# Gate and up projections as Strassen's seven half-size products, in two passes with partial results in DRAM

## What is computed

```python
x = x + (mix @ w_out[l]).astype(x.dtype)
x = x + swiglu(rmsnorm(x, norm2_w[l]), w_gate_up[l], w_down[l]).astype(x.dtype)
...
def swiglu(h, w_gate_up, w_down):
    gu = h @ w_gate_up
    gate, up = jnp.split(gu, 2, axis=-1)
    return (jax.nn.silu(gate) * up) @ w_down
```

## Time and profile before

| | us |
|---|---|
| median of 3 runs | 2583.36 (2579.16 to 2587.95) |
| the profiled execution | 2588.09 |
| its span, first to last instruction | 2586.3 |

### The profile page before, as it was taken

How to read it: one execution, slowest core, us unless ns; L and a number is a source line. 1 busy time by engine, 2 the same in 40 slices (tenths; PEclk the granted TensorE clock), 3 DMA queues, 4 the chain that set the end, 5 groups by cost and what they waited for, 6 DMA issues and landing times.

```text
span 2586.3 us, 36373 instructions
## 1 busy us (share of the span) xinstructions
PE 2475.5 (96%) x15138; PEld 2063.7 (80%) x15138; DVE 1193.8 (46%) x2105; ACT 558.7 (22%) x905; POOL 477.6 (18%) x162
## 2 busy tenths in 40 slices
PE   6899999998999999999999999989999999999998
PEld 6778888887788788888787877777778888888887
DVE  6884138873698523141622733663522222222224
ACT  4211111214321102141323434430210000000002
POOL 2100232230000132202210100000333333333330
PEclk8989999999999999999999999999999999999999
DMA  8544534236466833421333431123111111111101
GB/s 268 151 154 153 175 109 136 82 114 204 135 208 208 252 118 130 140 100 62 122 109 117 144 116 71 69 70 124 49 49 49 49 49 49 49 45 45 44 20 65
DMA packets 226899, 284.69 MB, mean 110 GB/s; under 512 B 31857, under 2 KB 144466, under 8 KB 226770
## 3 DMA queue, kind: packets, MB, share of 16 engines
q1 hardware_dynamic: 194370, 234.44, 28.2%
q10 hardware_dynamic: 32400, 48.38, 5.1%
HBM read 200.89 MB, written 81.89 MB: 109 GB/s over the span
## 4 chain that ended last, share of the span: by engine, by line
PE 82%; DVE 9%; DMA 3%; issue 3%; ACT 3%; SPq 1%; POOL 0%; ACTq 0%; DVEq 0%; POOLq 0%
PE PS L500 26%; PE PS L3127 19%; PE PS L503 16%; PE PS L3144 9%; DVE W_LO L409 1%; PE PS L1854 1%; PE PS L1834 1%; DMA LAR<-ret_d 1%; PE PS L682 1%; PE PS L2421 1%; PE PS L2416 1%; PE PS L1174 1%; DMA CB<-pch_d 1%; DVE XN L643 1%; PE PS L1295 1%
## 5 line engine op out<-in xcount | busy, mean ns | idle before, releaser
L442 POOL TENSOR_SCALAR W_HI<-RAW 128x2048 fp32r<-128x2048 f32 (+1 forms) x66 | 132.1, 2011 | 1507.7 <-PE PS L500 671.8
L500 PE MATMUL PS<-W_HI,OP_HI 128*128 128x512 f32 (+1 forms) x1184 | 310.2, 406 | 5.3 <-DVE XI L1458 2.9
L500 PE MATMUL PS<-W_LO,OP_HI 128*128 128x512 f32 (+1 forms) x1184 | 292.1, 389 | 0.0
L500 PE MATMUL PS<-W_HI,OP_LO 128*128 128x512 f32 (+1 forms) x1184 | 289.1, 387 | 0.0
L500 PEld LDWEIGHTS PS<-W_HI,OP_HI 128*128 128x128 f32 x1184 | 222.1, 196 | 53.7 <-issue 4.7
L500 PEld LDWEIGHTS PS<-W_LO,OP_HI 128*128 128x128 f32 x1184 | 223.2, 192 | 46.8 <-issue 0.5
L500 PEld LDWEIGHTS PS<-W_HI,OP_LO 128*128 128x128 f32 x1184 | 220.4, 189 | 44.6 <-issue 0.3
L3200 DVE TENSOR_TENSOR AB<-PS,GSB 128x512 f32<-128x512 f32 x44 | 30.4, 691 | 391.0 <-ACT GSB L3183 391.0
L529 ACT ACTIVATE OST<-PS 128x512 f32<-128x512 f32 (+2 forms) x164 | 91.2, 556 | 503.6 <-PE PS L503 269.1
L503 PE MATMUL PS<-OP_HI,W_HI 128*128 128x512 f32 (+1 forms) x768 | 190.8, 391 | 3.8 <-POOL W_HI L442 3.8
L503 PE MATMUL PS<-OP_HI,W_LO 128*128 128x512 f32 (+1 forms) x768 | 184.1, 382 | 0.3 <-DVE W_LO L409 0.3
(11 more groups left out here) (449 smaller groups left out, 3425.3 us busy)
## 6 DMA issues: line engine op xcount, KB each, us to landing
RAW<-in_w_in SPq DMA_DIRECT2D x28, 1024.0 KB, 5.9
RAW<-in_w_gate_up SPq DMA_DIRECT2D x44, 512.0 KB, 4.7
RAW<-in_w_out SPq DMA_DIRECT2D x12, 1024.0 KB, 8.9
RAWD<-in_w_down SPq DMA_DIRECT2D x11, 1024.0 KB, 4.9
X<-x_d SPq DMA_DIRECT2D x4, 2048.0 KB, 9.1
x_d<-X SPq DMA_DIRECT2D x2, 4096.0 KB, 16.5
ptok_d<-OST ACTq DMA_DIRECT2D x24, 256.0 KB, 2.0
pch_d<-OST ACTq DMA_DIRECT2D x24, 256.0 KB, 2.1
```

Of the source, the lines that this page charges most:

```text
L442: nc.gpsimd.tensor_scalar(hi, raw, 1.0, 1.0, ALU.mult, ALU.mult).then_inc(*w_hi.by(1))
L500: ins = nc.tensor.matmul(PS[:, bank, 0:width], act_part[:, k, (g.tile0 + a) * P:(g.tile0 + a + 1) * P], w_part[:, slot, k, 0:width], start ...
```

## The change

Gate and up are no longer computed as two products of full size. Of a block's weights, the gate and up columns (256 each) and the two halves of the contraction make a 2x2 matrix of blocks (`A11`, `A21` in rows 0 to 511, `A12`, `A22` in rows 512 to 1023), the activations another one (the two halves of the contraction, `K1` and `K2`, by the two halves of the tokens, `T1` and `T2`). Strassen's scheme in Winograd's form gets the four result blocks from seven products of half size. Each is 12 matmuls for each of the two column tiles `f`.

- First pass, over all 11 blocks: four products (regions 0 to 3 of `WRH`, `WRL`), 8 x 12 = 96 matmuls a block. Two of the weight operands are sums of blocks. The partial results, four kinds for each block, go to `spill_d` in DRAM, eight DMAs of 256 KB a block.
- Second pass, over all 11 blocks again, with the weights loaded again: three products, 6 x 12 = 72 matmuls a block, then the down product of 96 as before. All three weight operands are sums or differences of blocks, and the activations are three precomputed sums (`C1`, `C6`, `C7`, made in steps 1, 3, 5 and 7 of the first pass). The partial results are fetched back, four DMAs of 512 KB a block.
- DVE makes the sums of weight blocks in place in `RAW` (two or three of 128x1024), POOL rounds them to `WRH` (one of 128x1024 for each region), and DVE makes `WRL`, which POOL did before (`lo`). POOL also rounds `w_down`; DVE subtracts.
- A product's PSUM bank is copied by ACT, and a second product is then accumulated onto the same bank.
- The fifth normalization gets times of its own (`NORM5`). It subtracts one half of the features from the other, and six of its tiles are now transposed ahead of the first product of the layer, which is woven together with `out2`.

The diff, cut to what is spoken of:

```diff
+    NF = 2 * FFB
+    spill_d = scratch("spill_d", (4 * NF * P, HALF))
+    WRH, WRL = at("WRH", "whi", 16384, [P, 4, 4, 2 * P], F32R), at("WRL", "wlo", 16384, [P, 4, 4, 2 * P], F32R)
...
+    RAWD = at("RAWD", "ophi", 16384, [P, 2, D])
...
+    E_UP, E_GATE, UP1, GATE2 = range(4)
+    STEPS = 2 * FFB
+    SUM_TIMES = (1, 3, 5, 7)
...
     def sp_ffn(sp):
...
+        sp.wait_ge(*ff_lo(3))
+        load_half(1, 1)
+        for i in range(FFB):
+            sp.wait_ge(*ff_lo(region_no(i, 3)))
+            load_half(i + 1, 0)
+            for f in range(2):
+                sp.wait_ge(*ff_cp(8 * i + 3 + f))
+                store(UP1, i, f, UPC)
+            for f in range(2):
+                sp.wait_ge(*ff_q(4 * i + 1 + f))
+                store(E_UP, i, f, PRE)
+            sp.wait_ge(*ff_lo(region_no(i + 1, 2)))
+            load_half(i + 2, 1)
+            for f in range(2):
+                sp.wait_ge(*ff_cp(8 * i + 7 + f))
+                store(GATE2, i, f, GSI)
+                sp.wait_ge(*ff_q(4 * i + 3 + f))
+                store(E_GATE, i, f, POST)
+        sp.wait_ge(*products_done(FFB - 1, 6))
+        load_down(0)
+        for kind, tile in ((E_UP, LE1), (UP1, LUP), (GATE2, LGS), (E_GATE, LE2)):
+            sp.wait_ge(*ff_st[kind](16 * NF))
+            fetch(kind, 0, tile)
+        sp.wait_ge(*ff_lo(region_no(FFB, 2)))
+        load_half(FFB + 1, 0)
+        for i in range(FFB):
+            j = FFB + i
+            if i + 1 < FFB:
+                sp.wait_ge(*ff_wlo(i + 1))
+                load_down(i + 1)
+            if j + 2 < STEPS:
+                sp.wait_ge(*ff_lo(region_no(j + 1, 2)))
+                load_half(j + 2, 0)
+                load_half(j + 2, 1)
...
     def pool_ffn(pool):
+        def hi(j, r):
+            pool.wait_ge(*sums_done(j))
+            if j:
+                pool.wait_ge(*products_done(j - 1, 2 * r + 2))
+            else:
+                pool.wait_ge(*mm_done(gemms["out2"].first + 13))
+            G.tensor_scalar(WRH[:, r], region_source(j, r), 1.0, 1.0, ALU.mult, ALU.mult).then_inc(*ff_hi.by(1))
...
     def pe_ffn(pe):
+        def product(r, f, bank, hi, lo, ks, ts, clear):
+            for n, (w, x) in enumerate(((WRH, hi), (WRL, hi), (WRH, lo))):
+                for k in range(4):
+                    ins = nc.tensor.matmul(PS[:, bank, :], w[:, r, k, f * P:(f + 1) * P], x[:, ks + k, ts],
+                                           start=clear and n == 0 and k == 0, stop=n == 2 and k == 3, skip_group_check=not clear)
+            ins.then_inc(*ff_p.by(1))
...
     def dve_ffn(dve, chain):
...
+        def sums(j):
+            dve.wait_ge(*ff_raw[0](32 * (j + 1)))
+            dve.wait_ge(*ff_raw[1](32 * (j + 1)))
...
+        def lo(j, r):
+            dve.wait_ge(*ff_hi(region_no(j, r)))
+            V.tensor_tensor(WRL[:, r], region_source(j, r), WRH[:, r].bitcast(F32), SUB).then_inc(*ff_lo.by(1))
...
+        for j in range(FFB):
+            T = ff_time(j)
+            if j:
+                yield T + 0.3
+                lo(j, 3)
...
+            yield T + 1.7
+            sums(j + 1)
+            yield T + 2.3
+            lo(j + 1, 0)
+            yield T + 2.45
+            lo(j + 1, 1)
+            for f in range(2):
+                yield T + 2.7 + 0.5 * f
+                dve.wait_ge(*ff_cp(8 * j + 5 + f))
+                chain(V.tensor_tensor(POST[:, f, :], PRE[:, f, :], POST[:, f, :], ADD))
+                V.tensor_tensor(PRE[:, f, :], PS[:, f, :], POST[:, f, :], SUB).then_inc(*ff_q.by(1))
+            yield T + 3.35
+            lo(j + 1, 2)
...
+        for i in range(FFB):
+            j = FFB + i
+            T = ff_time(j)
...
+            V.tensor_tensor(WD_LO[:, :, :], RAWD[:, :, :], WD_HI[:, :, :].bitcast(F32), SUB).then_inc(*ff_wlo.by(1))
+            if i == 0:
+                yield T + 0.95
+                sums(j + 1)
...
+            for f in range(2):
+                yield T + 1.5 + 0.5 * f
...
+                dve.wait_ge(*products_done(j, 3 + f))
+                V.tensor_tensor(LE1[:, f, :], PS[:, f, :], LE1[:, f, :], ADD).then_inc(*ff_c11.by(1))
...
+                V.tensor_tensor(LE1[:, f, :], LE1[:, f, :], LUP[:, f, :], ALU.mult).then_inc(*ff_ab.by(1))
+                if f == 0 and j + 1 < STEPS:
+                    yield T + 2.25
+                    lo(j + 1, 1)
+                yield T + 2.15 + 0.4 * f
+                dve.wait_ge(*ff_ahi(4 * i + 1 + f))
+                V.tensor_tensor(A_LO[:, f, T1], LE1[:, f, :], A_HI[:, f, T1].bitcast(F32), SUB).then_inc(*ff_alo.by(1))
+            for f in range(2):
...
+                chain(V.tensor_tensor(LE2[:, f, :], PS[:, 2 + f, :], LE2[:, f, :], ADD))
+                V.tensor_tensor(LE2[:, f, :], LE2[:, f, :], LGS[:, f, :], ALU.mult).then_inc(*ff_ab.by(1))
...
+                V.tensor_tensor(A_LO[:, f, T2], LE2[:, f, :], A_HI[:, f, T2].bitcast(F32), SUB).then_inc(*ff_alo.by(1))
+                if f == 0 and j + 1 < STEPS:
+                    yield T + 3.3
+                    lo(j + 1, 2)
+            if i + 1 < FFB:
+                for v in range(15):
+                    yield T + 3.3 + 0.25 * v
+                    add(i, v)
+                    if v == 9 and j + 2 < STEPS:
+                        yield T + 5.6
+                        sums(j + 2)
...
+    NORM5 = (10.2, 11.2, 12.2, 13.2, 14.2, 15.2, 15.7, 16.7)
```

More of the change, by code:

```diff
@@ new lines, in region_source, with spill, load_half, load_down @@
+    def region_source(j, r):
+        return ((A21, A22, A12, A11) if first_part_of(j) else (A11, A12, A21))[r]
+    def spill(kind, f, n):
+        row = (kind * NF + f) * P
+        return spill_d[row:row + n * P, :]
+    def sp_ffn(sp):
+        def load_half(j, half):
+            i = j % FFB
+            for m in range(2):
+                src = wgu[half * HALF:(half + 1) * HALF, i * 256 + m * FF:i * 256 + m * FF + 256]
+                sp.dma_start(RAW[:, half, :, m * 256:(m + 1) * 256], src.rearrange("(k p) n -> p k n", p=P))\
+                  .then_inc(*ff_raw[half].by(16))
+        def load_down(i):
+            sp.dma_start(RAWD[:, :, :], wdn[i * 256:(i + 1) * 256, :].rearrange("(k p) n -> p k n", p=P))\
+              .then_inc(*ff_raw[2].by(16))
+        def store(kind, i, f, tile):
+            sp.dma_start(spill(kind, 2 * i + f, 1), tile[:, f, :]).then_inc(*ff_st[kind].by(16))
+        def fetch(kind, i, tile):
+            sp.dma_start(tile[:, :, :], spill(kind, 2 * i, 2).rearrange("(f p) n -> p f n", p=P))\
+              .then_inc(*ff_ld[kind].by(16))
+        sp.wait_ge(*w_split(len(halves)))
+        load_half(0, 0)
+        load_half(0, 1)
+        sp.wait_ge(*ff_lo(3))
[33 more added lines that the diff above has]
+            if i + 1 < FFB:
+                sp.wait_ge(*ff_alo(4 * i + 2))
+                fetch(E_UP, i + 1, LE1)
+                fetch(UP1, i + 1, LUP)
+                sp.wait_ge(*ff_alo(4 * i + 4))
+                fetch(GATE2, i + 1, LGS)
+                fetch(E_GATE, i + 1, LE2)
@@ L3115, in pool_ffn @@
+        for r in range(3):
+            hi(0, r)
+        for j in range(FFB):
+            hi(j, 3)
+            for r in range(3):
+                hi(j + 1, r)
+        for i in range(FFB):
+            j = FFB + i
+            pool.wait_ge(*ff_raw[2](16 * i + 16))
             if i:
@@ L3166, in pe_ffn @@
[L3166 to L3191 removed]
+                pool.wait_ge(*products_done(FFB, 0))
@@ L3209, in add @@
             V.tensor_tensor(X[:, t, c * HALF:(c + 1) * HALF], X[:, t, c * HALF:(c + 1) * HALF],
-                            PS[:, 4 + v % 4, :], ALU.add).then_inc(*ff_x.by(1))
-        dve.wait_ge(*xn_turned(turned_base(5) + TT))
-        with dve.Fori(0, FFB - 1) as i:
-            gate(i)
-            for v in range(16):
-                add(i, v)
-        gate(FFB - 1)
+                            PS[:, 4 + v % 4, :], ADD).then_inc(*ff_x.by(1))
+        yield 10.3
+        sums(0)
+        for r, time in enumerate((13.35, 13.75, 14.75, 15.65)):
+            yield time
+            lo(0, r)
```

402 lines of the change are left out of this document (282 added, 120 removed), and 2 rows, old and new, of the table SHARED.

## The result

The changed kernel takes 2602.06 us (median of 5 runs, 2595.43 to 2603.66) against 2583.36 before; the ratio is 1.0062, 95% interval 1.0047 to 1.0077. It is slower by 0.6%, where I had forecast 2576 us, faster by 0.3%. The time lies 1 us above my range of 2550 to 2601.

The account below looks back on a forecast made before the run. PE, busy 96% of the span, was taken as the bound. Terms -59.8 - 8 + 4 + 21 + 35 = -7.8 us took the profiled 2586.3 to 2578.5; allowing for the 2583.36 median, the forecast was 2576 us, range 2550 to 2601.

Parts of the forecast that it names:

- Beginning, -8: Start of the layer: POOL no longer subtracts there, so `XN` is not held up; 8 us saved, 2 of 10.0 kept.
- Arithmetic, -59.8: Eleven blocks: 264 matmuls fewer at 0.2267 us each save 59.8 us, if PE still never waits.
- First pass, +4 (0 to 15): First pass: the load loop of 22.1 us against 21.76 makes each step wait 0.4 us, 4 us over 11.
- The loop 13.9 + 3p: First pass, from step start until `ff_q` lets the next step start: 13.9 us + 3p, p the us for 1 MB.
- one of the rivals (0.13, 2598 us): First pass bound by its load loop: at p = 3.3 a step waits 2.1 us, 23 in all; chance 0.13.
- 1.8 + 3p = 10.0 us: Loop's middle: two 1 MB loads and 1 MB of spills, 3p = 8.2 us, then 1.8 us until landed.
- 8.4: Loop's last part: sums, two roundings, two `lo`, additions and hand-overs until `ff_q`, 8.4 us.
- 3.7: Loop's first part: from step start through partial results, rounding and `lo` to SP's issue of loads, 3.7 us.
- Port in the first pass: First-pass loop: two POOL roundings, 2.10 us, hold the port that DVE operations with two SBUF inputs need.
- Turn, +21 (14 to 26): First step of second pass: waits of 19.6 us before the first down product and 1.9 before down tile 4.
- Later steps, +35: Nine later second-pass steps: waits before down tiles 0 and 4, 3.9 us each step, 35 us (26 to 39).
- Clock: Rival: PE's clock falls after the wait for tile 4, 1.8 us for nine steps, +16, 2592 us; chance 0.13.

Follow-up runs that it names:

- e10: Changed kernel with only orders changed, on SP and VectorE, in first pass, turn and second pass; 2517.88 us, ratio 0.9747 to the kernel before.
- e8: Changed kernel with the four stores of the second half of a first-pass step issued by ScalarE into its own queue; 2581.92 us.
- e1: Changed kernel with the four GATE2 and E_GATE stores of a first-pass step queued on SP behind the next load of half 0; 2572.07 us.
- e2: Changed kernel with ScalarE, not GpSimd, rounding the WRH regions of steps 1 to 10 in the first pass; 2587.73 us.

## Why the prediction was wrong

- *Beginning, -8:* -11, of which 10 are the two waits and what follows them. Right in sign and near in size by luck, since the mechanism was wrong: not `XN`.
- *Arithmetic, -59.8:* as said; e10 shows it whole.
- *First pass, +4 (0 to 15):* +25. **This is the step that failed.** The loop 13.9 + 3p was right in shape, and one of the rivals (0.13, 2598 us) carried its consequence. Its middle term was mis-sized: 1.8 + 3p = 10.0 us measured 12.2 (1966.54 to 1978.76), and 8.4 measured 9.05, while 3.7 measured 2.34. I gave SP's issues no length and so counted 3 MB at full rate from the first issue; at 142 and 267 GB/s the first 4 us fall short of that. Half 0 waits for `lo(j, 3)`, which I had not put on the path, and then another 1.05 us for the stores' issues (e8), and it lands behind their bytes, 8.8 us after its issue for 6.0 in e1, where no store stands ahead of it. For the 1.8 us from the last byte to the landing the prediction names no row, and no run takes it apart from the rest. I also left `UPC`'s stores out, and what the matmuls lose behind the waits, 5.8 us over the pass. The rival's reason, p = 3.3, is not what happened: from 1970.5 on DMA moves 336 to 383 GB/s, as in the earlier trace rows.
- The limit of about 358 GB/s from the Trainium skill (DMA: Bandwidth & Descriptors, Specifications) gives the loop 0.93 us a step too much, 9 to 10 us over the pass. The 2 us stretches of 366, 383 and 391 GB/s lie above it, loads and stores together, and what the pass lost was not the rate of transfers under way but their order and the collision.
- *Port in the first pass:* I had the two roundings on the loop and not the third, which joins them when the sums are late and holds the pair of `lo` to 4.04 us for 2.28. e2 shows that this alone would have been enough to wait little.
- *Turn, +21 (14 to 26):* +24.7, inside its range. The wait was 20.39 us for 19.6, the load landing 23.5 us into the step for 20.7. The rest is what the matmuls lose behind the waits of 3.62 and 20.39 us (42.39 - 38.08 = 4.3 us, mostly half pace), which I had not put there; the 1.9 us ahead of tile 4 did not come.
- *Later steps, +35:* +34.4, 41.90 us for 42.0, with the port's share of 0.9 measured as 0.78.
- *Clock:* I gave 0.13 to a fall behind the wait for tile 4. It didn't fall there. It fell behind the wait for tile 0 in four steps of nine, swallowed by the wait for tile 4 as I had said, and in the first pass and at the turn, where nothing swallowed it.

What failed was one term, and with 25 instead of 4 us in it the sum gives +13 against -8. That is 21 of the 26 us between forecast and median. The other 5 are the choice of execution: the profiled one before took 4.7 us more than its median, the one after is the median itself.

## What to carry to other kernels

Where loads feed a loop and stores share their queue, lay the queue out with the issues' own lengths, and put stores whose buffers have a step of time behind the next load. A twelfth fewer matmuls in a layer is only had if the orders of the queues beside PE are written from PE's due times back: here the same instructions took 2602 or 2518 us. A short idle time of PE costs twice when the clock falls behind it and no later wait takes up the loss, so one wait of 2.65 us was dearer than two of 1.84 and 1.43. And being late can bring a collision that being on time avoids: the third rounding stood beside the two `lo` with the sums 14.6 us into the step, and not with the sums at 8.7.
